# Recurrence of an RWKV-7 layer: five masked matrices made in one go on GpSimd, in six buffers instead of two

## The reference, cut to what matters

```
def step(state, inp):
    r_t, w_t, k_t, v_t, kk_t, a_t = inp
    sk = jnp.einsum('bhij,bhj->bhi', state, kk_t)
    state = (state * w_t[:, :, None, :]
             - sk[..., None] * (kk_t * a_t)[:, :, None, :]
             + v_t[..., None] * k_t[:, :, None, :])
    y = jnp.einsum('bhij,bhj->bhi', state, r_t)
    return state, y
```

## Time and profile before

| | us |
|---|---|
| median of 3 runs | 3374.06 (3373.85 to 3381.95) |
| the profiled execution | 3377.38 |
| its span, first to last instruction | 3375.6 |
| PE busy over the span | 2849.1 (84%) |
| DVE busy | 1487.0 (44%) |
| POOL busy | 1476.3 (44%) |

### The profile page before, as it was taken

One profiled execution on the slowest core, in us unless ns is written; L12 is line 12 of the kernel. 1 busy time (PEld: TensorE's weight loads), 2 busy tenths in 40 slices (PEclk: granted clock), 3 DMA queues, 4 the chain that ended last, 5 costly groups with the idle time before them and its releaser, 6 DMA issues. The chain is left out here.

```text
span 3375.6 us, 59409 instructions
## 1 busy us (share of the span) xinstructions
PE 2849.1 (84%) x25224; PEld 2331.9 (69%) x25224; DVE 1487.0 (44%) x1823; ACT 922.1 (27%) x1632; POOL 1476.3 (44%) x817
## 2 busy tenths in 40 slices
PE   0787887989999997699835688888857999999999
PEld 0565666777878885477623588878856788878887
DVE  5654334764434344422243355555531543434344
ACT  2335433212222222121133233333322422222221
POOL 3232234333444442555543465556524544444443
PEclk9889998999999999899967899999988999999999
DMA  5421233563323331354423311111123223323333
GB/s 191 160 75 38 88 112 107 191 220 107 99 88 98 96 94 38 92 130 127 123 62 69 88 47 52 58 53 47 47 52 106 88 89 105 95 93 99 95 100 119
DMA packets 207763, 323.86 MB, mean 96 GB/s; under 512 B 126112, under 2 KB 126240, under 8 KB 207520
## 3 DMA queue, kind: packets, MB, share of 16 engines
q1 hardware_dynamic: 107680, 295.12, 28.3%
q10 hardware_dynamic: 99840, 25.17, 3.3%
HBM read 285.71 MB, written 33.55 MB: 95 GB/s over the span
## 5 line engine op out<-in xcount | busy, mean ns | idle before, releaser
L649 POOL TENSOR_TENSOR wl<-w,wh 128x1024 fp32r<-128x1024 f32 x320 | 778.0, 2438 | 1201.7 <-ACT wh L685 1201.5
L213 PE MATMUL ps<-hi,wh 128*128 128x512 f32 x1824 | 737.3, 404 | 49.6 <-POOL wl L649 43.3
L214 PE MATMUL ps<-lo,wh 128*128 128x512 f32 x1824 | 722.3, 396 | 0.0
L215 PE MATMUL ps<-hi,wl 128*128 128x512 f32 x1824 | 721.8, 396 | 0.0
L685 ACT ACTIVATE wh<-w 128x1024 fp32r<-128x1024 f32 x320 | 337.6, 1057 | 696.7 <-DMA w<-in_ffn_w_in 539.1
L905 DVE SCALAR_TENSOR_TENSOR xt<-ps,mod,xt 128x512 f32<-128x512 f32 x384 | 286.5, 750 | 448.6 <-PE ps L215 448.5
L213 PEld LDWEIGHTS ps<-hi,wh 128*128 128x128 f32 x1824 | 350.9, 192 | 136.6 <-POOL wl L649 43.5
L214 PEld LDWEIGHTS ps<-lo,wh 128*128 128x128 f32 x1824 | 350.7, 192 | 74.7 <-issue 3.5
L215 PEld LDWEIGHTS ps<-hi,wl 128*128 128x128 f32 x1824 | 349.7, 192 | 75.6
L213 PE MATMUL ps<-act_hi,wh 128*128 128x512 f32 x704 | 279.2, 397 | 13.9 <-DVE act_lo L914 11.6
L215 PE MATMUL ps<-act_hi,wl 128*128 128x512 f32 x704 | 277.9, 395 | 0.0
(11 more groups left out here) (215 smaller groups left out, 4536.7 us busy)
## 6 DMA issues: line engine op xcount, KB each, us to landing
w<-in_ffn_w_in SPq DMA_DIRECT2D x176, 512.0 KB, 3.7
piece<-in_ada_w SPq DMA_DIRECT2D x96, 512.0 KB, 4.8
w<-in_ffn_w_out SPq DMA_DIRECT2D x88, 512.0 KB, 3.6
w_raw<-in_w_rkv SPq DMA_DIRECT2D x48, 512.0 KB, 4.1
scratch<-stage ACTq DMA_DIRECT2D x96, 256.0 KB, 2.9
w<-in_wqk SPq DMA_DIRECT2D x20, 512.0 KB, 4.5
xt<-in_xT SPq DMA_DIRECT2D x4, 2048.0 KB, 11.2
w<-in_attn_w_out SPq DMA_DIRECT2D x16, 512.0 KB, 3.6
```

The lines of the kernel that those rows point to most:

```text
L213: pe.matmul(out, w_hi(k), x_hi(k), start=first and k == 0, stop=False)
L214: pe.matmul(out, w_hi(k), x_lo(k), start=False, stop=False)
L215: ins = pe.matmul(out, w_lo(k), x_hi(k), start=False, stop=last and k == kc - 1)
L649: pool.tensor_tensor(wl[n % NW][:, :, :], wr[n % NW][:, :, :], wh[n % NW][:, :, :].bitcast(F32), ALU.subtract).then_inc(*wlo.up)
```

## The change

`ntm` becomes six buffers, one for each level. POOL then makes the pieces of levels 1 to 5 of chunk y in a row at the start of y's period, and only behind them takes the keys of x. The piece of level 0 stays where it was. The wait of a mask is now on the product of the same level of the chunk before. PE reads `ntm[l]` instead of `ntm[l % 2]`. Nothing is computed in another way, and the number of instructions on each engine is the same.

```diff
-                ntm = [st(f"n_t_level{b}") for b in range(2)]
+                ntm = [st(f"n_t_level{l}") for l in range(len(LEVELS))]
...
-                            pool.wait_ge(*g["x_done_w"].at(2 * NL * ch + 2 * l - 2))
+                            pool.wait_ge(*g["x_done_w"].at(max(2 * NL * (ch - 1) + 2 * l + 2, 0)))
                             m = con[:, C_LEVEL + l * CHUNK:C_LEVEL + (l + 1) * CHUNK].unsqueeze(1).to_broadcast(W8)
-                            pool.tensor_tensor(ntm[l % 2][:, :, :], nt[:, :, :], m, ALU.mult).then_inc(*g["lev_mask"].up)
+                            pool.tensor_tensor(ntm[l][:, :, :], nt[:, :, :], m, ALU.mult).then_inc(*g["lev_mask"].up)
...
                         def period(x, y, zz):
+                            for l in range(1, NL):
+                                level_mask(y[0], l)
                             for l in range(NL):
-                                if l < NL - 1:
-                                    level_mask(y[0], l + 1)
-                                elif x is not None:
+                                if l == NL - 1 and x is not None:
                                     level_mask(x[0], 0), first_inverse(*x)
...
-                                    ins = pe.matmul(quarter(q)[hs, j, :], ntm[l % 2][hs, jj, :],
+                                    ins = pe.matmul(quarter(q)[hs, j, :], ntm[l][hs, jj, :],
```

## The result

The changed kernel took 3410.85 us, median of 4 runs (3401.80 to 3417.81), against 3375.53 us for the kernel before (4 runs): a ratio of 1.010, 95% interval 1.0071 to 1.0128, or 35 us slower. Run again later beside other kernels it came out at 1.0088 (1.0074 to 1.0102), 29 us slower. I had forecast slower by 17 us, 3391.5, in a range from 3380 to 3400. The direction was right, the size half of what was measured.

What follows compares the result with a forecast made beforehand. PE sets the pace, with mask waits of 40.0 us in 13 periods. 13 x 1.4 = 18.2 us, minus 0.8, adds 17.4 to the profiled 3377.38; less 3.3 for the median gives 3391.5 us, range 3380 to 3400.

Steps and rivals of the forecast that it cites:

- What goes: PE's level 2 mask wait, 1.22 us a period, goes; level 1's 1.86 stays; at most 15.9 of 40.0 us.
- The turns of DVE and POOL: In DVE's `begin`, DVE and POOL alternate, 0.55 and 1.12 us a turn; the scan ends 2.14 us late.
- the list of signs: Expected timeline: `k` about 1.75, scan about 2.3, masks of levels 2 to 4 at 1.7, period 38.9 us.
- The rival in which the scan isn't held: Only `k` is held by a mask; outputs 0.3 us late, 3 us slower, 3377 us; chance 8%.
- the one in which DVE keeps its run: DVE keeps its turn through `kk`, `k` and scan; 13 us faster, 3361 us; chance 6%.
- the one in which POOL runs through: POOL runs five masks without letting DVE in; outputs 4.1 us late, 53 us, 3427 us; chance 3%.
- The new wait for `rn`: PE waits for `rn` ahead of `outputs`, which start at 2096.87 instead of 2095.49, 1.4 us late.
- The stall's size: Each middle period gets 1.4 us longer, 38.9 instead of 37.49; 13 times, 18.2 us.
- Keys moved and hidden: POOL's keys of the next chunk start later, about 2094.3, with 3 to 4 us of cover left; cost nothing.
- The edges: Outside the middle periods: chunk 1 gains 0.8 us, chunks 0 and 15 are put at 0.
- the sum: Whole run: 13 x 1.4 = 18.2, minus 0.8, is 17.4 us slower; forecast 3391.5 us.

Runs made afterwards that it cites:

- the repeat: The changed kernel, unaltered, measured and profiled a second time: 3407.08 us, 1.0088 against the kernel before.
- the full filling: Changed kernel with PE doing the level 1 product three times and 24 small products more in the level 1 mask wait: 3388.72 us, 1.0034 against the kernel before.
- three variants of this kernel: Masks of levels 2 to 5 behind DVE's scan (1.0002); only two masks ahead of the keys (1.0040); six buffers, old mask order, new waits (1.0079).
- the delayed kernel before: Kernel before, masks and buffers untouched, with four short reductions added on DVE behind the scan: 3418.78 us, 1.0128 against the kernel before.
- The filling experiments: Changed kernel with repeated PE products in its waits: norms product three times (1.0071), level 1 product three times (1.0047), the latter plus 24 small products (1.0034).
- norms thrice: Changed kernel in which PE does the product of norms three times over in its wait ahead of `level_t`: 3401.23 us, 1.0071 against the kernel before.

## Why the prediction was right on the direction and half the size

- **What goes.** Right. The level 2 wait went and the level 1 wait stayed.
- **The turns of DVE and POOL.** Right in the working: `k` 1.75, scan 2.28, the second to fourth masks 1.72, 1.71 and 2.18 (the list of signs had 1.7 for the fourth too, which the working itself doesn't give: that mask waits for the scan), `level_t` 2.14 us later in its wait (0.36 to 2.50). The rival in which the scan isn't held, the one in which DVE keeps its run and the one in which POOL runs through are out by these rows. So the engines don't meet only at semaphores, as I had put it at the start: these two hold each other up with none between them. The Trainium skill ("SBUF — State Buffer", section "Who interferes with whom") has a DVE instruction with two SBUF inputs and a GpSimd one that reads SBUF shut each other out; the held scan agrees (2.28 against 1.21).
- **The new wait for `rn`.** Right: 0.4 in the mean of the 13 periods.
- **The stall's size.** Right: 38.87 in the changed kernel where half clock is hidden or, in the repeat, absent, 38.88 with the full filling, against 37.49: 1.4 a period, 18 us.
- **Keys moved and hidden.** Right in the changed kernel, where the wait at level 3 stays 0.91. But I looked only for who waits for the keys. I didn't ask what a shifted POOL queue would meet on DVE in level 3; in three variants of this kernel that decided.
- **The edges.** From the first `kk` to the first middle one 1.2 us went, against the 0.8 put.
- **The step that failed: the sum.** It took PE's products at their durations of before, so it put TensorE's clock at no cost without a reason, and no rival had them slower. In the changed profile the 13 periods take 29.4 us more (516.8 from level 1 mask to level 1 mask, against 487.4): 18 of the stall, which I had, and 11.5 of half clock, 8 periods at 1.3 to 1.5. (The whole profile is only 24.4 us longer, since 3.0 less passed before the recurrence, 1.2 less at the edges and some 0.9 less behind.) The full filling, which takes the stretches away and leaves the stall, and the delayed kernel before, which has them without the masks, show that this is a cost of its own that follows from holding PE up.
- **What stays open.** The four runs of the result are 26 to 42 us above the kernel before, and only the fastest of them has a trace. The repeat's trace lies at the middle of its five runs (3406.46 us), and 12 middle periods take 28.6 us more in it than in the kernel before, which is nearly all of its 29. The 6 us between its 29 and the first 35 have no trace; whether those runs had more of their half-clock stretches on the path wasn't seen. The filling experiments say that it isn't PE's waits alone, but they don't give the rule by which the clock falls.

## What to carry to other kernels

POOL work that is put back to back isn't free when it only fills idle time: count the DVE instructions with two SBUF inputs beside it, and give each a full turn of the POOL instruction. Look for POOL's idle time at a place where DVE has none of them, and treat a wait that seems useless as something that may keep the two apart. When a change makes PE wait longer in a tight loop, work the time out twice, at whole clock and with a stretch of half clock in each round.

## What the runs showed of the hardware that I had not expected

- In the middle periods the granted clock was 1.00 in the kernels with periods of 35.70, 37.45 and 37.49 us. It fell to half for a few us at a time in those whose periods at whole clock are 38.15, 38.28 and 38.87 and in the delayed one (39.0 where the stretch is hidden), with no wait of PE over 2.73 us. The length of the period doesn't decide by itself: the full filling has 38.88 and a whole clock. 0.7 us of delay on PE (38.15) cost 0.56 more in clock (38.71). The Trainium skill ("TensorE: Matmul & The Clock Gate", section "Part 1: The HAM clock gate (the "warmup" mystery)") says that the clock follows how busy PE has been. By PE's busy time these traces agree only in part: 87% in a period of before, whole; 88% in one of the kernel with norms thrice, and the clock fell 2.3 us behind its end.
- What fills PE's waits matters, though the runs don't tell in which respect. Four records of large products more a period (128x512, 1.9 us) left a half-clock stretch in every second period, as did 64 records of small ones in the same wait; with 112 records, the 48 further ones in the other wait, none was left. Whether their number or their place did it wasn't tried, nor were large ones in both waits.
- DVE and POOL took turns one instruction each when both had two-input work in SBUF queued, also in the middle of a run on either side, as expected. No row of before had a held scan; here it took its turn 13 times of 13 (2.28 us in the mean instead of 1.21). A DVE instruction of 128x512 then took 1.75 instead of 0.68, and a POOL one 1.7 instead of 1.26.
